# One load for the last whole and the half block of down weights, row halves in turn in the first mixer, and the second mixer's gates in two column groups

## What is computed

```python
for layer in range(2):
    xn = rms_norm(h, norm_mix_g[layer])
    if layer == 0:      # first mixer
        proj = xn @ ab_w_in
        y_a = gla_group(proj[..., :GLA_COLS], ...)     # 4 heads, keys of 64
        y_b = rwkv7_group(proj[..., GLA_COLS:], ...)   # 8 heads of 64, chunks of 16 tokens
    else:               # second mixer
        proj = xn @ cd_w_in
        lru_x, lru_g, m_x, m_o, m_if = split_cols(proj, CD_SIZES)   # m_if: 2 x 4 gate columns
        y_a = rglru_group(lru_x, lru_g, ...)
        y_b = mlstm_group(m_x, m_o, m_if, ...)
    h = h + concatenate([y_a, y_b]) @ w_mix_out[layer]
    h = h + memory_cross_attention(rms_norm(h, ...), mem_n, wq, wkv, wo)
    h = h + conv_glu_ffn(rms_norm(h, ...), w_up, ..., w_down)   # w_down has 2752 rows = 21 x 128 + 64
```

## Time and profile before

| | us |
|---|---|
| median of 3 runs | 2265.56 (2265.2 to 2265.84) |
| the profiled execution | 2268.09 |
| its span in the trace | 2266.2 |
| PE busy | 2127.8 |
| PE weight loads busy | 1413.8 |
| DVE busy | 619.3 |
| ACT busy | 370.2 |
| DMA: mean rate over the span | 259 GB/s |

### The profile page before, as it was taken

How to read it: one execution, slowest core, us unless ns; L and a number is a source line. 1 busy time by engine, 2 the same in 40 slices (tenths; PEclk the granted TensorE clock), 3 DMA queues, 4 the chain that set the end, 5 groups by cost and what they waited for, 6 DMA issues and landing times.

```text
span 2266.2 us, 25809 instructions
## 1 busy us (share of the span) xinstructions
PE 2127.8 (94%) x10764; PEld 1413.8 (62%) x10764; DVE 619.3 (27%) x1229; ACT 370.2 (16%) x672; POOL 125.3 (6%) x186
## 2 busy tenths in 40 slices
PE   9999999999999999999999999996789999999765
PEld 6887788888888888888877753332334333433222
DVE  4344432334454224336225321000001010100001
ACT  4321122100014222000222320100001000001000
POOL 0113300000000000000000010100000000001000
PEclk9999999999999999999999999998889999999888
DMA  6321053444632445336533459999999999999997
GB/s 252 112 75 38 2 208 115 151 161 156 237 149 101 159 149 223 149 140 271 235 146 112 188 222 402 428 427 427 427 427 420 425 428 427 426 392 428 427 428 281
DMA packets 44427, 587.54 MB, mean 259 GB/s; under 512 B 5344, under 2 KB 5616, under 8 KB 9104
## 3 DMA queue, kind: packets, MB, share of 16 engines
q1 hardware_dynamic: 44304, 585.82, 63.8%
HBM read 584.75 MB, written 1.05 MB: 258 GB/s over the span
## 4 chain that ended last, share of the span: by engine, by line
PE 73%; DMA 24%; DVE 1%; ACT 1%; issue 1%; SPq 0%; PEld 0%; DVEq 0%; ACTq 0%; PEldq 0%
PE pb L410 72%; DMA kv<-in_gu 7%; DMA ring<-in_gu 6%; DMA ring<-in_dne 6%; DMA kv<-in_dne 2%; DMA arena<-in_dne 2%; PE pb L420 1%; DMA arena<-in_gu 1%; DVE arena L327 1%; ACT arena L371 0%; DVE arena L312 0%; DMA ht<-in_x 0%; DVE arena L321 0%; ACT arena L377 0%; DMA ring<-in_dn 0%
## 5 line engine op out<-in xcount | busy, mean ns | idle before, releaser
L410 PE MATMUL pb<-arena,ring 128*128 128x256 f32 (+1 forms) x2816 | 614.1, 380 | 4.9 <-ACT arena L371 2.0
L410 PEld LDWEIGHTS pb<-arena,ring 128*128 128x128 f32 (+1 forms) x2816 | 522.6, 188 | 89.4 <-issue 8.7
L410 PE MATMUL pb<-arena 128*128 128x256 f32 (+12 forms) x2644 | 491.3, 383 | 34.0 <-DMA ring<-in_dne 16.6
L410 PEld LDWEIGHTS pb<-arena 128*128 128x128 f32 (+5 forms) x2644 | 317.7, 168 | 194.1 <-issue 158.9
L410 PE MATMUL pb<-arena,cst 128*64 128x512 f32 (+6 forms) x1032 | 338.0, 617 | 58.6 <-DMA kv<-in_gu 40.8
L410 PE MATMUL pb<-ring,cst 128*64 128x512 f32 (+2 forms) x800 | 341.3, 628 | 0.0
L410 PEld LDWEIGHTS pb<-arena,cst 128*64 128x64 f32 (+4 forms) x1032 | 104.6, 140 | 265.4 <-issue 262.8
L410 PE MATMUL pb<-ring,arena 128*64 128x512 f32 (+2 forms) x480 | 192.1, 619 | 7.3 <-DMA arena<-in_dne 7.3
L377 ACT ACTIVATE arena<-pb 128x512 f32<-128x512 f32 (+4 forms) x123 | 68.7, 559 | 550.8 <-PE pb L420 420.4
L319 DVE TENSOR_SCALAR arena<-pb 128x512 f32<-128x512 f32 x30 | 20.8, 692 | 466.6 <-PE pb L410 466.6
L410 PEld LDWEIGHTS pb<-ring,cst 128*64 128x64 f32 (+2 forms) x800 | 100.0, 140 | 67.6 <-issue 67.6
(11 more groups left out here) (145 smaller groups left out, 1472.3 us busy)
## 6 DMA issues: line engine op xcount, KB each, us to landing
arena<-in_gu SPq DMA_DIRECT2D x60, 2048.0 KB, 18.6
ring<-in_gu SPq DMA_DIRECT2D x50, 2048.0 KB, 19.4
arena<-in_dne SPq DMA_DIRECT2D x33, 2048.0 KB, 19.4
ring<-in_dne SPq DMA_DIRECT2D x21, 2048.0 KB, 19.4
kv<-in_gu SPq DMA_DIRECT2D x18, 2048.0 KB, 19.4
ring<-in_up SPq DMA_DIRECT2D x13, 2048.0 KB, 7.8
ring<-in_wkv SPq DMA_DIRECT2D x8, 2048.0 KB, 7.8
ring<-in_dn SPq DMA_DIRECT2D x8, 2048.0 KB, 7.6
```

The costliest lines, as they stand in the source:

```text
L410: r = self.e.matmul(out, lhsT, rhs, start=start, stop=stop, skip_group_check=True)
```

## The change

Three things, in one edit:

1. `pack_rows` puts the turned 64 rows behind the last whole block, so dn0.5 is one load of 1536 columns (768 KB). `LOADS` has dn0.5 where dn0.6 was, and one load fewer; `half_rows_p` reads the same unit and frees nothing. The same for dn1.
2. First mixer: the matmuls on the two row halves are issued in turn (lora w2 with a2, `gla.sc`, `gla.st` 0 with 1, the chunk pairs); `outputs` makes both output tiles in one place, all 128-row matmuls first and the 64-row ones in turn behind them. ACT and DVE read the tiles in the new order.
3. Second mixer: DVE adds the squares (`added_v`, three additions) and PE sums them with two matmuls instead of eight; four steps of side work stand ahead of that sum; the 16 gate matmuls go over the channels with the input gates in columns 0 to 3 and the forget gates in 32 to 35 in turn, and the bias `bf` moves to partitions 32 to 35.

```diff
+        turned = np.concatenate([tail[:, :n], tail[:, n:]])
+        out[-1] = np.concatenate([out[-1].reshape(128, -1), turned], axis=1).reshape(-1)
...
-dn0.2 ada.2 dn0.3 ada.3 dn0.6 dn0.4 dn0.5 wkv1.0 cd_if cd.0 cd_m.0 cd.1 cd_m.1 wkv1.1 wkv1.2 wkv1.3 mixo1.0
+dn0.2 ada.2 dn0.3 ada.3 dn0.5 dn0.4 wkv1.0 cd_if cd.0 cd_m.0 cd.1 cd_m.1 wkv1.1 wkv1.2 wkv1.3 mixo1.0
...
-            w = P.unit(unit)[:, 0:512]
+            w = P.unit(unit)[:, D:D + 512]
...
-            P.used(unit)
...
-            lora_out_p(P, "w2", SML[1][0:64])
-            lora_out_p(P, "a2", SML[1][64:128])
+            lora_out_p(P, ("w2", SML[1][0:64]), ("a2", SML[1][64:128]))
...
+            def outputs():
...
+                for h2, b in enumerate(bs):
+                    for q2 in range(2):
...
+                            P.mm(b[:, o0:o0 + 128], gv[:, i, hd * 128:(hd + 1) * 128], gsc[:, h2, q2 * 2 + i, :],
+                                 q2 + i == 0, False)
                 for q2 in range(2):
...
+                    for c in (1, 2, 3):
+                        for h2, b in enumerate(bs):
...
-            proj_p(P, "ab_r.2", "rkv.v", after_first=lambda: outputs(0))
-            outputs(1)
+            proj_p(P, "ab_r.2", "rkv.v", after_first=outputs)
...
-                for hh in range(2):
-                    pr = half64[hh]
-                    b = P.tile(f"{n}.w{hh}")
-                    for o0, lhs in ((0, KK), (256, K)):
-                        P.mm(b[:, o0:o0 + 128], lhs[pr, j, ts_], EP[pr, j, ts_], True, True)
-                        P.mm(b[:, o0 + 128:o0 + 256], lhs[pr, j, ts_], R[pr, j, ts_], True, True,
-                             sig=f"{n}.w{hh}" if o0 else None)
-                    b = P.tile(f"{n}.a{hh}")
+                bw = [P.tile(f"{n}.w{hh}") for hh in range(2)]
+                for o0, lhs, rhs in ((0, KK, EP), (128, KK, R), (256, K, EP), (384, K, R)):
+                    for b, pr, hh in zip(bw, half64, range(2)):
+                        P.mm(b[:, o0:o0 + 128], lhs[pr, j, ts_], rhs[pr, j, ts_], True, True,
+                             sig=f"{n}.w{hh}" if o0 == 384 else None)
+                ba = [P.tile(f"{n}.a{hh}") for hh in range(2)]
+                for b, pr, hh in zip(ba, half64, range(2)):
                     P.mm(b[:, 0:128], EP[pr, j, ts_], KK[pr, j, ts_], True, True, sig=f"{n}.a{hh}")
...
-            sum_p(P, "n1")
+            P.beside(kv_p(P, 1))
+            P.fill("m1.fs", 4)
+            added_p(P, "n1")
...
-            for q in range(2):
-                for c in range(8):
-                    P.wait_ge(f"n1.x{c // 2}")
-                    P.mm(b[0:4, q * 256:(q + 1) * 256], w[:, c, q * 4:q * 4 + 4], XT[:, c, :], c == 0, c == 7,
+            for c in range(8):
+                P.wait_ge(f"n1.x{c // 2}")
+                for q in range(2):
+                    P.mm(b[32 * q:32 * q + 4, 0:256], w[:, c, q * 4:q * 4 + 4], XT[:, c, :], c == 0, c == 7,
...
+            added_v(V, "n1")
             root_v(V, "n1")
```

More of the change, by code:

```diff
@@ L874, in down_p @@
                 if last and halves is not None:
-                    half_rows_p(P, acc, halves, f"{unit}.{len(groups)}", f"{n}.g{len(groups)}", ready(whole))
+                    half_rows_p(P, acc, halves, f"{unit}.{gs[-1]}", f"{n}.g{len(groups)}", ready(whole))
                 parts = []
@@ L1066, in front_p @@
             P.wait_ge("lora_v")
-            lora_out_p(P, "g2", SML[3])
+            lora_out_p(P, ("g2", SML[3]))
             proj_p(P, "ab_r.1", "rkv.k")
             P.wait_ge("load const16")
[L1070 to L1078, removed]
+            bs = [P.tile(f"gla.sc{par}") for par in range(2)]
+            P.wait_ge("gla.dec")
+            for j in range(2):
+                for i in range(2):
+                    o0 = (j * 2 + i) * 128
+                    for par, pr in enumerate(half64):
+                        P.mm(bs[par][:, o0:o0 + 128], gkinv[pr, j, i * 128:(i + 1) * 128],
+                             gq[pr, j, i * 128:(i + 1) * 128], True, True,
                              sig=f"gla.sc{par}" if j + i == 2 else None)
@@ L1092, in front_p @@
             proj_p(P, "ab_r.0", "rkv.r", after_first=lambda: heads("rw.h", "rw.sq", BE))
-            for c in range(3):
-                b = P.tile(f"gla.st{c}")
+            for cs in ((0, 1), (2,)):
+                bs = [P.tile(f"gla.st{c}") for c in cs]
                 P.wait_ge("free gla.kt", "free gla.v1")
-                r0, i = 64 * (c % 2), c // 2
                 for j in range(2):
-                    P.mm(b[:, j * 256:(j + 1) * 256], gkt[r0:r0 + 64, i, j * 128:(j + 1) * 128],
-                         gv[r0:r0 + 64, i, j * 256:(j + 1) * 256], True, True, sig=f"gla.st{c}" if j else None)
@@ L1101, in outputs @@
-            def outputs(h2):
-                b = P.tile(f"gla.o{h2}")
-                P.wait_ge("free gla.sc1", "free gla.st2")
-                for q2 in range(2):
[L1105 to L1114, removed]
-                            P.mm(b[:, q2 * 256 + c * 64:q2 * 256 + c * 64 + 64], gst[p0:p0 + 64, j, c, :],
-                                 gq[p0:p0 + 64, j, c * 64:(c + 1) * 64], False, c % 2 == 1,
-                                 sig=f"gla.o{h2}" if end else None)
@@ L1150, in front_s @@
                 S.free(f"gla.qk{j}")
-            for w, dst, nb in (("w2", SIG, NEG["w0"]), ("a2", A, NEG["a0"])):
-                for j in (0, 2):
+            ranks = (("w2", SIG, NEG["w0"]), ("a2", A, NEG["a0"]))
+            for j in (0, 2):
+                for w, dst, nb in ranks:
                     b = S.tile(f"rw.{w}{j}")
@@ L1157, in front_s @@
                     S.free(f"rw.{w}{j}")
+            for w, dst, _ in ranks:
                 if w == "w2":
@@ L1573, in chunk_pair @@
                     V.free(f"{n}.w{hh}")
+                for hh in range(2):
                     b = V.tile(f"{n}.a{hh}")
@@ L3389, in block @@
                 if what in ("dn0", "dn1"):
[L3390 to L3391 removed]
+                    at = int(n) * 4 * 128 * D
+                    size = 4 * D if int(n) < 5 else D + 512
                     return [(0, 128, dram[what][at:at + 128 * size].rearrange("(p n) -> p n", p=128))]
```

32 lines of the change are left out of this document (20 added, 12 removed).

## The result

| | before | after |
|---|---|---|
| median, same call (4 runs each) | 2265.70 us (2265.20 to 2266.44) | 2250.18 us (2249.46 to 2251.92) |
| the profiled execution | 2268.09 | 2251.92 |
| its span in the trace | 2266.2 | 2250.1 |

The ratio is 0.9932, with a 95% interval of 0.9915 to 0.9950: the changed kernel is 0.7% or 15.5 us faster. The forecast was 2249.2, the range 2243.5 to 2254.5.

The account below looks back on a forecast made before the run. PE was taken to set the first 1377 us, with the expert-weight stream following it. The gains summed to 16.3 us, from 2268.1 to 2251.8 by the profile, 2249.2 by the median; range 2243.5 to 2254.5.

Parts of the forecast that it names:

- Rival E: The expert stream's start hangs on something other than PE, so the change does nothing, 2265 us; chance 4%.
- (a): First mixer, lora w2 and a2: 16 records issued in turn take 2.0 us instead of 2.90; gain 0.95 us.
- (b): First mixer, scores: 16 records of 128 columns in turn take 1.13 us instead of 1.71; gain 0.56 us.
- (d): First mixer, outputs: one group of 3.35 us replaces two totalling 7.0; gain 3.65 us, 2.3 if 64-row records don't pair.
- (g): First FFN's down weights: PE's 1.61 us wait for dn0.5's load goes; gain 1.65 us, 0.2 if dn0.4 comes late.
- (h): Second mixer: sum and gates end 2.55 us earlier; with 3.45 from the shorter drain, 6.0 us in all.
- Rival D: Four-column groups don't run side by side, costing 0.9 us, time 2250.1 us; chance 5%.
- (f): First mixer, eight chunk pairs: PE's records 0.78 us shorter each, but DVE takes most back; gain 1.8 us of 6.3.
- (e): Clock fall at 127.99 us behind the second output group, taken to come from its row changes, goes; gain 1.7 us.
- rival C: The clock fall stays or another takes its place, 1.7 us each; time 2250.9 to 2252.6 us; chance 15%.
- Rival B: DVE is not in the way of the chunk pairs: they gain 6.3 us instead of 1.8, time 2244.7 us; chance 12%.
- Rival F: Slower: PE's idle 0.66 us in each chunk-pair tick brings clock falls; sixteen cost 27 us, giving 2276 us; chance 3%.

Follow-up runs that it names:

- e8: Changed kernel with both gates in columns 0 to 3, in two column ranges of the bank, so they can't run side by side; profiled time 2254.39 us.
- e3: Kernel before the change with only the outputs of the linear attention put in one group; profiled time 2264.38 us.
- e6: Kernel before the change with only the last whole block and the half block of the down weights as one load; profiled time 2265.98 us.
- e7: Kernel before the change with only the second mixer's part (added squares, four steps of side work ahead, gates in two column groups); profiled time 2258.75 us.
- e9: Changed kernel with only DVE's order in the chunk pairs changed, copies ahead of masks and of the older pair's addition; median 2250.31 us, ratio 0.9929 to kernel before.
- e10: Changed kernel with DVE's copies first and PE's wait for the A masks moved behind its side work step; median 2248.88 us, ratio 0.9923 to kernel before.
- e4: Changed kernel with the outputs back in their old form and places, two groups with 16 row changes; profiled time 2262.88 us.

## Why the prediction was right, and where it wasn't

- *PE sets the first 1377 us and the stream follows it.* Right: the stream came 17.9 us earlier with PE. Rival E falls.
- *The price of a record side by side, 8 x 0.216 + 0.27.* Right to 0.1 us in all of its uses: (a) 1.92 against 2.0, (b) 1.09 against 1.13, the pairs 1.32 against 1.34. For groups of four columns e8 shows that they run side by side. The differences in the sum were less careful: 2.90 less 2.0 is 0.90 and not 0.95 in (a), and 1.71 less 1.13 is 0.58 and not 0.56 in (b).
- *(d), (g), (h).* Right to 0.1 us, each alone in e3, e6 and e7. The tie between DVE's additions and the side work came out as a wait of 0.15, where 0.25 to spare was forecast. In (d) the split into 0.107 a record and 0.175 a change was a guess from one row. Another split, 64-row records of 0.05 not side by side and 0.26 a change, fits the old and the new group as well. The starts in the trace decide for the guess: the pairs come every 0.105 us, and single 64-column records in the old group every 0.11.
- *Rival D's price, 0.9.* Wrong, though the rival didn't happen: e8 cost 3.0. Each piece of XT would need 8 x 0.216 = 1.73 on PE against DVE's 1.03, so the loss comes in all four pieces and not in the last alone. D's time would have been about 2252.2, still in the range.
- *(f) DVE takes back most of the pairs' gain.* Right in mechanism, shown by e9 and e10: the same PE program with DVE's operations in another order gains 2.3 us more, and 4.2 more with the late wait. The size, 1.8, was too high by 0.5. The step that failed is the 0.4 for each of the three pairs without the plain pattern. The first gained nothing (DVE's copy took 0.80 there and X was as late as before), the last two 0.45 and 0.21. I had also put PE's whole loss at one wait of 0.9 for X; it is two, of about 0.3 for the A masks and 0.3 to 0.5 for X, since the older wait stands ahead of the side work.
- *(e) The clock fall at 128 belongs to the second group of outputs.* In this pair of traces the 1.78 came as forecast, but the reason was too strong. The fall can stand behind the first group or be missing with the same instructions. Four in six times 1.7, about 1.1, is what the runs support, and rival C's point, that other falls come and go, held as well: one in the trace after against two before, and one to four over the experiments' traces, one of them (e4) twice as long. All that begin at 688 to 705, 1098 to 1114 and 1208 to 1219 stand at the end of a wait of PE, those at 128 and at 1321 to 1340 don't. So some falls come with waits, and the one that the prediction was about doesn't.
- Rival B (the pairs gain in full) didn't happen, and e10 shows what most of it takes. Rival F (clock falls in the first mixer from PE's short holes) had no sign: none of the 14 traces has a fall between 140 and 680 us.

That the profiled execution met the forecast to 0.1 us (2251.92 against 2251.8) was luck in part: 2.3 us from other falls and 1.8 lost in the stream were both not forecast and nearly cancel; the rest is 0.5 too much for the pairs and 0.2 of a later start. The median is 1.0 us above the forecast of 2249.2. That is less than the interval of the ratio leaves open (4 us either way), so it is not put down to any step.

## What to carry to other kernels

When PE's stage gets shorter, look for the first wait behind it on the other engine, and for the operations on that engine that stand ahead of it without being needed: here two copies and a wait in another place were worth three times, in that stage, what the shorter matmuls were (4.2 against 1.3 us). What they would be worth without the shorter matmuls was not run. Half-height and narrow matmuls are priced by what already runs in turn elsewhere in the same trace. A change of a few microseconds is judged stage by stage in two traces; the total carries clock falls of 0.7 to 1.7 us each and up to 5.6 us of the stream, which come and go between executions of the same program.

## What the runs showed of the hardware

- The granted clock of TensorE falls to 0.50 (1.2 GHz) for 3.4 us also where PE has no wait ahead or during it: behind the old outputs (128.0, 127.8, 116.4, 117.4), and, in seven traces, at 1321 to 1340, behind 8 records on 32 rows. The 32 records at 116.08 in e4 took 8.86 instead of 7.17.
- The other falls ahead of the stream begin between 0.4 us before and 1.4 us behind the end of a wait of PE: the 1.42 near 700 (eleven of the fourteen traces), the 2.00 near 1100 (five), the 0.97 near 1208 to 1219 (three). The same waits stand in the other traces without a fall, so from one execution to the next it comes or not.
- Records of 64 rows and 64 columns in turn on the two halves run side by side: 24 in 1.5 us in the changed kernel, a pair every 0.105 us, where single ones come every 0.11. A change between 128 and 64 rows costs 0.16 to 0.19 more, an estimate from these spacings and the two groups (3.54 us with 8 changes, 3.43 with 2).
- Column groups of four columns, 0 to 3 and 32 to 35, run side by side as halves of 64 do: 8 records of 256 columns a piece kept up with DVE's 1.03 us, and without the groups the gates took 3.0 us more (e8).
- Where a fall stands matters, by one pair of places: one ahead of a transfer that leads was covered (1879.0 before), one behind it cost 1.4 us (1869.8 after: 8.5 us from 1870.31 to the transposes, 7.0 before).
